# A two-block transformer kernel: nine of the memory's key and value products in rounded parts, and the convolution's sum one product later

## The chip, the cores and the metric

The kernel runs on one core of one Trainium2 chip. The metric is the device time of one execution in microseconds (us). TensorE (PE) multiplies, VectorE (DVE) and ScalarE (ACT) work elementwise, SyncE (SP) issues the weights' DMAs. PSUM has eight banks of 128 x 512 floats.

## The reference, cut to what matters

Two blocks of a model of width 1024 on 512 tokens. The first has two layers, each with a mixer, a cross attention to a memory of 256 tokens, and a SwiGLU FFN. The change lies in a layer where the mixer ends and the memory's keys and values are computed:

```
y_att  = mla_group(...)                 # 8 heads, chunk-causal softmax, heads of 64
y_conv = conformer_conv_group(...)      # GLU, depthwise conv of 31 taps, LayerNorm over 512 channels, silu
x = layer_norm(ALPHA * x + concat([y_att, y_conv]) @ mix_w_o, ...)
kv = (mem @ xa_w_kv).reshape(B, M, 2, XA_HEADS, XA_HEAD_DIM)   # mem: 256 x 1024, xa_w_kv: 1024 x 2048
k, v = kv[:, :, 0], kv[:, :, 1]
```

All in float32. The second block (a gated delta network and 16 experts) is not touched.

## The kernel before

Everything is feature-major: a tensor of 1024 features and n tokens is 8 tiles of 128 partitions by n. The order of the work on each engine is written out by hand; engines meet through counting semaphores (`signal`), one step for each instruction of a kind.

**Rounded products.** A plain float32 matmul is two records in the trace. Most large products of the kernel are instead made of three matmuls in the rounded type fp32r: weights and inputs are split in a high part (a copy that rounds) and a low part (the difference), and `split_product` adds high x high, high x low and low x high for each of the 8 k. Here the split weights are made by ACT (high) and DVE (low).

**The stage.** In each layer PE runs a loop over 8 heads. For head h: `turn_probs(h, (0, 1))`, the scores of head h + 2, in some heads `modulation_rows` (a small product for the second block, weights streamed through the ring), `turn_probs` of tiles 2 and 3, in even heads `sums_across` (the reciprocals of the softmax sums of two heads, spread to bank 4), then `values(h)`. ACT takes the exponentials of head h + 1 ahead of head h's evictions (`turned_probs`, L2558), and copies bank 4 to mixT (L2573). DVE takes the maxima (`maximum`), the reciprocals, and between them single taps of the depthwise convolution (`convolve(n)`: 4 x 31 = 124 taps a layer, L3352, the first of each tile L3349). Product 0 of the memory stands in head 6.

After the heads PE runs `memory_product(1)` to `(11)` (`product`, L1197): products 0 to 7 give the key tiles (128 features x 256 memory tokens), 8 to 11 the values (two token tiles by 512, 512, 512 and 256 columns; the last 256 come later). Between them stand `conv_sum` (behind product 6; it needs all 124 taps), `conv_variance` (behind 8) and the spread of the reciprocal (behind 9, L1218). Then comes `residual(0, ...)`, the output projection by mix_w_o, in rounded parts: its inputs `m_split` are made of mixT by DVE (`split_half`, attention half and convolution half), its weights by `high(n)` on ACT (L2612) and `low(n)` on DVE (L3211).

**Memory.** `ring` has three slots; the key and value weights are chunks 10, 11 and 12 (`C_XKV`), which SP loads when PE has given slots back (`give_back`, `used`). In layer 0 the last of four modulation rows gives back three slots at once. The last value weights, `w_vlast`, go to the arena behind the last head. `raw`, slot 2, takes the chunks of mix_w_o once product 7 is done.

Of the kernel before, what the change touches and what calls it, by code (L numbers as in the profile page):

```python
# [80 lines left out]
RING_MODS = (4, 5)  # L81
LATE_MODS = {(0, 1): 4, (0, 2): 5, (1, 1): 5}
# [5 lines left out]
MIX_SPLIT = 2 * (CT - 1) + 4  # L88
HALF = FT // 2
# [102 lines left out]
def build(nc, A, out, debug=None):  # L192
    with ExitStack() as ctx:
# [146 lines left out]

        kr_raw = probsT[:, 0, :]
# [95 lines left out]
        mw_hi, mw_lo = signal("split_weights_hi", MIX_SPLIT + SPLIT_CHUNKS), signal("split_weights_lo", MIX_SPLIT + SPLIT_CHUNKS)  # L437
        f_hi, f_lo = mw_hi.after(MIX_SPLIT), mw_lo.after(MIX_SPLIT)
# [451 lines left out]

        def norm_banks(i):

            return (2, 3, 4, 5, 4) if i == 2 else (0, 1, 2, 6, 7)
# [237 lines left out]
        def _(pe):  # L1131
# [46 lines left out]
            for l in range(DEPTH):  # L1178
# [79 lines left out]
                def split_product(bank, weights, rhs, n, need):  # L1258

                    for k in range(n):  # L1260
                        need(k)
                        for wp, rp in ((0, 0), (0, 1), (1, 0)):
                            mm = pe.matmul(bank[:, :], weights(wp, k), rhs(rp, k), start=(k == 0 and wp == rp),  # L1263
                                           stop=(k == n - 1 and wp == 1))
                            if k == 0 and wp == rp:
                                say_spent(mm)
# [10 lines left out]
                def residual(i, n0, rhs, ready):  # L1277


                    for t in range(KT):  # L1280
                        if t >= 4:
                            pe.wait_ge(z_ok.sem, z_ok.at(l, i * KT + t - 3))
                        split_tile(ps[(6, 7, 4, 5)[t % 4]], n0, t, rhs, ready).then_inc(res_mm.sem, 1)
# [219 lines left out]
                def memory_product(n):  # L1503
# [30 lines left out]
                for h in range(HEADS):  # L1534
# [3 lines left out]
                    if 1 <= h < RING_MODS[l]:  # L1538
                        modulation_rows(h)
# [8 lines left out]
                    if h < RING_MODS[l]:  # L1548
                        modulation_turn(h)
# [3 lines left out]
                for n in range(1, 12):  # L1553
# [3 lines left out]
                    if n == 6:  # L1557
# [812 lines left out]
        def _(act):  # L2370
# [37 lines left out]
            for l in range(DEPTH):  # L2408
# [151 lines left out]

                act.wait_ge(kcopy.sem, kcopy.at(l, 1))
                exps(0)
                for h in range(HEADS):
# [3 lines left out]
                    if h < RING_MODS[l]:  # L2567
                        act.wait_ge(mod_rows.sem, mod_rows.at(l, h + 1))
                        A1(gates[:, h % 2, 0:P], mod_row(l, h)[:, 0:P], ACT.Copy).then_inc(mod_row_ev.sem, 1)
                    turned_probs(h, (2,))  # L2570
                    if h % 2 == 0:
                        act.wait_ge(rec_mm.sem, rec_mm.at(l, h // 2 + 1))
                        A1(mixT[:, h // 2, :], ps[4][:, :], ACT.Copy).then_inc(rec_ev.sem, 1)  # L2573
                    turned_probs(h, (3,))
# [53 lines left out]

                for n in range(1, 12):
                    memory_copy(n)  # L2630
                    if n == 6:
# [3 lines left out]
                    if n == 9:  # L2635
                        conv_silu()
                    if n == 9:
                        high(0)

                high(1)  # L2640
# [523 lines left out]
        def _(dve):  # L3164
# [31 lines left out]
            for l in range(DEPTH):  # L3196
# [20 lines left out]
                def add_in(i, t):  # L3217
                    dve.wait_ge(res_mm.sem, res_mm.at(l, i * KT + t + 1))
                    V.scalar_tensor_tensor(out=zT[:, t, :], in0=xT[:, t, :], scalar=ALPHA,
                                           in1=ps[((6, 7, 0, 1) if i == 2 else (6, 7, 4, 5))[t % 4]][:, :],  # L3220
# [39 lines left out]
                def add_shifted(i, t):  # L3260
# [13 lines left out]
                    bank = ps[((6, 7, 0, 1) if i == 2 else (6, 7, 4, 5))[t % 4]][:, :]  # L3274
# [118 lines left out]
                for t in range(CT):  # L3393
# [5 lines left out]
                    convolve(6 if t < CT - 1 else 16)  # L3399
# [49 lines left out]

                for h in range(HEADS):  # L3450
# [567 lines left out]
```

## Time and profile before

| | us |
|---|---|
| runs | 2459.09 median of 3 (2456.24 to 2461.99) |
| profiled execution | 2459.64, its span 2457.8 |
| TensorE busy | 2406.1 (98%) |
| VectorE busy | 1245.3 (51%) |
| ScalarE busy | 792.1 (32%) |
| mean granted TensorE clock | 0.996 of full speed |

The page also gives the chain of work that ended last, followed back from the last instruction. The groups by form tell one shape of an instruction from another, with count, busy time and mean. The timeline merges neighbouring instructions of a line; in brackets stands the idle time of the engine before them and what ended it. Times are from the span's start. PE is matmuls, PEld weight loads; the end of a matmul is modelled, so that starts are the better measure of its pace.

### The profile page before, as it was taken

What the parts mean: (1) busy time and instruction counts of PE and PEld (TensorE: products, weight loads), DVE (VectorE), ACT (ScalarE), POOL (GpSimd) and SP (SyncE); (2) the same over time, 40 slices, a digit from 0 to 9 for tenths busy, and PEclk for the clock granted to TensorE, in tenths of its full rate; (3) what the DMA queues carried; (4) which work ended last, traced back from release to release, by engine and by line L of the source; (5) the groups of instructions that cost most, each with busy time, mean ns of one, the idle gap of its engine ahead of it and who ended that gap; (6) DMA issues with size and microseconds to landing.
All of it is one profiled execution on the core that took longest, in us unless ns stands there. A gap on an engine that the chain in (4) does not pass through costs nothing.

```text
span 2457.8 us, 35670 instructions
## 1 busy us (share of the span) xinstructions
PE 2406.1 (98%) x15406; PEld 1721.0 (70%) x15406; DVE 1245.3 (51%) x1826; ACT 792.1 (32%) x1284; POOL 173.5 (7%) x117
## 2 busy tenths in 40 slices
PE   9999999999999999999999999999999999999998
PEld 6566877888887757687788888787899754444332
DVE  6884746433336887555633434687566431112122
ACT  4452534222224353343422322526333441111111
POOL 0000000000000000000000000190344010000000
PEclk9999999999999999999999999999999999999999
DMA  4352222323334233322332322211100289999998
GB/s 171 98 180 95 75 97 69 96 85 104 103 110 141 65 138 138 103 69 90 100 97 83 112 88 84 95 70 69 37 3 3 104 321 426 427 426 426 427 427 342
DMA packets 248819, 380.70 MB, mean 155 GB/s; under 512 B 21945, under 2 KB 187094, under 8 KB 224982
## 3 DMA queue, kind: packets, MB, share of 16 engines
q1 hardware_dynamic: 248316, 378.31, 41.9%
q8 instruction: 122, 2.00, 0.3%
q14 instruction: 35, 0.29, 0.0%
q10 hardware_dynamic: 346, 0.11, 0.0%
HBM read 376.28 MB, written 2.10 MB: 154 GB/s over the span
## 4 chain that ended last, share of the span: by engine, by line
PE 89%; DMA 6%; DVE 2%; ACT 2%; SPq 1%; issue 1%; DVEq 0%; ACTq 0%
PE banks L1263 41%; PE banks L2242 10%; PE banks L1197 6%; PE banks L1752 4%; PE banks L1896 4%; DMA ring<-in_w_gate 3%; PE banks L1246 2%; PE banks L2088 2%; PE banks L1617 1%; PE banks L1250 1%; PE banks L1591 1%; DMA arena<-in_w_gate 1%; PE banks L1432 1%; PE banks L2188 1%; PE banks L2226 1%; PE banks L1495 1%
## 5 line engine op out<-in xcount | busy, mean ns | idle before, releaser
L2612 ACT ACTIVATE w_hi<-ring 128x2048 fp32r<-128x2048 f32 (+1 forms) x100 | 174.5, 1745 | 424.0 <-PE banks L1263 424.0
L1263 PE MATMUL banks<-ffn_x_hi,w_lo 128*128 128x512 f32 x640 | 249.2, 389 | 0.0
L1263 PE MATMUL banks<-ffn_x_lo,w_hi 128*128 128x512 f32 x640 | 249.2, 389 | 0.0
L1263 PE MATMUL banks<-ffn_x_hi,w_hi 128*128 128x512 f32 x640 | 249.2, 389 | 0.0
L3211 DVE TENSOR_TENSOR w_lo<-ring,w_hi 128x2048 fp32r<-128x2048 f32 (+1 forms) x96 | 198.7, 2069 | 63.0 <-ACT w_hi L2612 61.8
L3352 DVE SCALAR_TENSOR_TENSOR arena<-arena,taps 128x512 f32<-128x512 f32 x240 | 174.0, 773 | 1.1
L3572 DVE TENSOR_TENSOR squares<-gates,banks 128x512 f32<-128x512 f32 x44 | 30.3, 688 | 275.5 <-PE banks L1263 262.3
L1263 PE MATMUL banks<-ffn_hidden_hi,w_hi 128*128 128x512 f32 x352 | 138.5, 393 | 0.0
L1263 PEld LDWEIGHTS banks<-ffn_x_lo,w_hi 128*128 128x128 f32 x640 | 120.2, 188 | 24.9
L1263 PEld LDWEIGHTS banks<-ffn_x_hi,w_lo 128*128 128x128 f32 x640 | 120.2, 188 | 24.9
L1263 PEld LDWEIGHTS banks<-ffn_x_hi,w_hi 128*128 128x128 f32 x640 | 120.2, 188 | 24.8
L1263 PE MATMUL banks<-ffn_hidden_hi,w_lo 128*128 128x512 f32 x352 | 137.2, 390 | 0.0
L1263 PE MATMUL banks<-ffn_hidden_lo,w_hi 128*128 128x512 f32 x352 | 137.1, 390 | 0.0
L3968 DVE SCALAR_TENSOR_TENSOR gates<-gates,tap_rows,banks 128x512 f32<-128x512 f32 x16 | 12.0, 747 | 227.6 <-PE banks L2242 196.4
L2242 PE MATMUL banks<-arena,zT 128*64 128x512 f32 x448 | 103.0, 596 | 2.1 <-DMA arena<-in_w_gate 1.0
L2242 PE MATMUL banks<-ring,zT 128*64 128x512 f32 x432 | 98.5, 597 | 2.5 <-DMA ring<-in_w_gate 2.0
L1197 PE MATMUL banks<-arena,ring 128*128 128x256 f32 (+1 forms) x352 | 98.0, 438 | 0.0
L1896 PE MATMUL banks<-arena 64*64 64x64 f32 x2688 | 87.3, 222 | 0.7 <-ACT arena L2883 0.7
L1197 PEld LDWEIGHTS banks<-arena,ring 128*128 128x128 f32 x352 | 66.7, 190 | 30.4 <-issue 24.2
L1896 PEld LDWEIGHTS banks<-arena 64*64 64x64 f32 x2688 | 83.4, 137 | 5.0 <-issue 1.5
L2242 PEld LDWEIGHTS banks<-arena,zT 128*64 128x64 f32 x448 | 30.6, 137 | 65.1 <-issue 58.3
L1263 PEld LDWEIGHTS banks<-ffn_hidden_lo,w_hi 128*128 128x128 f32 x352 | 66.1, 188 | 14.0 <-issue 0.5
(571 smaller groups left out, 4695.4 us busy)
## 6 DMA issues: line engine op xcount, KB each, us to landing
ring<-in_ffn_w_in SPq DMA_DIRECT2D x88, 512.0 KB, 4.8
arena<-in_w_gate SPq DMA_DIRECT2D x28, 1024.0 KB, 21.1
arena<-in_w_up SPq DMA_DIRECT2D x28, 1024.0 KB, 21.4
ring<-in_w_gate SPq DMA_DIRECT2D x27, 1024.0 KB, 22.3
ring<-in_w_up SPq DMA_DIRECT2D x27, 1024.0 KB, 21.5
ring<-in_w_down SPq DMA_DIRECT2D x24, 1024.0 KB, 17.5
arena<-in_w_down SPq DMA_DIRECT2D x24, 1024.0 KB, 20.3
ring<-in_w_mod SPq DMA_DIRECT2D x18, 1024.0 KB, 7.0
```

The lines of the kernel that those rows point to most:

```text
L1197: mm = pe.matmul(bank[0:m, 0:width], weights(k), rhs(k), start=(k == 0), stop=(k == n - 1))
L1246: pe.matmul(ps[outs[o]][:, :], weights(o, wp, k), rhs[0][:, k, :], start=(k == 0 and wp == 0), stop=False)
L1250: mm = pe.matmul(ps[outs[o]][:, :], weights(o, 0, k), rhs[1][:, k, :], start=False, stop=(k == KT - 1))
L1263: mm = pe.matmul(bank[:, :], weights(wp, k), rhs(rp, k), start=(k == 0 and wp == rp), stop=(k == n - 1 and wp == 1))
L1752: mm = pe.matmul(out, wt[:, k, :], z[:, k, :], start=(k == 0 and i == 0), stop=(k == KT - 1 and i == 2))
L1896: mm = pe.matmul(units_of(bank)[rows, un, :], lhsT(un, rows), rhs(un, rows), start=True, stop=True)
L2088: mm = pe.matmul(bank, w_parts[wp], r_parts[rp], start=(k == DH and wp == rp), stop=(k == DH - 1 and wp == 1))
L2242: mm = pe.matmul(out, tokens, weights[:, n * 512:(n + 1) * 512], start=first, stop=last)
L2612: nc.scalar.activation(hi[:, 0:m], raw[n % 2][:, 0:m], ACT.Copy).then_inc(f_hi.sem, 1)
L3211: ins = V.tensor_tensor(lo[:, 0:m], raw[n % 2][:, 0:m], hi[:, 0:m].bitcast(F32), ALU.subtract)
L3352: ins = V.scalar_tensor_tensor(out=acc, in0=x, scalar=c, in1=acc, op0=ALU.mult, op1=ALU.add)
L3572: V.tensor_tensor(whole, gates[:, t % 2, :], ps[2 * (t % 4) + 1][:, :], ALU.mult)\
```

## The change

Products 1 to 7 (keys) and 8 and 9 (the first 512 value columns) become rounded products of three parts. The memory (`mem_x`, 2048 elements a partition) and eleven pieces of the weights (1024 each, `mem_part(1)` to `(11)`; piece 0 stays plain) are split: ACT makes the high parts (`memory_high`), DVE the low ones (`memory_low`, `memory_x_low`). The low parts lie on the raw weights in the ring, the high ones where the latents, queries and keys of the heads were and in zT, where the probabilities were. The value pieces' high parts lie on those of products 1 to 3. Since `m_split` lies on the memory's parts, `split_half(0)` goes behind product 9 on DVE.

Around it: `conv_sum` and the squares go from behind product 6 to behind product 7. In even heads tile 2 is turned ahead of the modulation rows, with `sums_across` and ACT's copy of bank 4; at head 6 this puts them ahead of product 0. In layer 0 modulation rows 3 go from head 3 to head 4 (`ROW_HEADS`). DVE takes the reciprocal of head h - 1 ahead of head h's maxima. Its taps: 7 more before the head loop, 2 instead of 4 in heads 5, 6 and 7, then 7 and 18 instead of 13 and 13. ACT makes the memory's high part in head 5, between the evictions of tiles 2 and 3, and pieces 1 and 2 in head 6. The projection's banks are 4, 6, 7, 5 instead of 6, 7, 4, 5, each with its own wait (`mixed_bank`); ACT makes `high(0)` ahead of `conv_silu` and `high(1)` ahead of product 11's eviction.

```diff
@@ new
+ROW_HEADS = ({0: 0, 1: 1, 2: 2, 4: 3}, {0: 0, 1: 1, 2: 2, 3: 3, 4: 4})
+        mem_x = [nc.alloc_sbuf_tensor_at(f"memory_{part}", [P, KT, MEM], F32R, offset=arena_at + 4 * lo).ap()
+                 for part, lo in (("hi", 0), ("lo", 12 * S))]
+        def res_bank(i, t):
+            return ((4, 6, 7, 5), (6, 7, 4, 5), (6, 7, 0, 1))[i][t % 4]
@@ PE, memory_product
-                    if n < 8:
+                    if 1 <= n < 8:
+                        pe.wait_ge(mem_lo.sem, mem_lo.at(l, n + 1))
+                        parts = mem_part(n)[1:]
+                        mm = split_product(bank, lambda i, k: parts[i][:, k], lambda i, k: mem_x[i][:, k, :], KT, lambda k: None, MEM)
+                    elif n < 8:
                         mm = product(bank, lambda k: wkv[:, k, (n % 4) * P:(n % 4 + 1) * P], lambda k: memT[:, k, :], width=MEM)
+                    elif n < 10:
+                        t = n % 2
+                        mm = split_product(bank, lambda i, k: mem_x[i][:, k, t * P:(t + 1) * P],
+                                           lambda i, k: (mem_v_hi, mem_w_lo[2])[i][:, k, :], KT,
+                                           lambda k: pe.wait_ge(mem_lo.sem, mem_lo.at(l, 8 + k // 2 + 1)))
@@ PE, heads
-                    if 1 <= h < RING_MODS[l]:
-                        modulation_rows(h)
+                    if h % 2 == 0:
+                        turn_probs(h, (2,))
+                        sums_across(h // 2)
+                    if h and h in ROW_HEADS[l]:
+                        modulation_rows(ROW_HEADS[l][h])
                     if h == HEADS - 2:
                         pe.wait_ge(sc_exp.sem, sc_exp.at(l, (HEADS - 1) * ST + 1))
                         memory_product(0)
-                    turn_probs(h, (2,))
-                    if h % 2 == 0:
-                        sums_across(h // 2)
+                    if h % 2:
+                        turn_probs(h, (2,))
                     turn_probs(h, (3,))
@@ PE, products
-                    if n == 6:
+                    if n == 7:
                         conv_sum()
@@ PE, projection
-                pe.wait_ge(mod_in.sem, mod_in.at(l, RING_MODS[l]))
-                pe.wait_ge(xkv_ev.sem, xkv_ev.at(l, 12))
-                residual(0, N_MO, m_split, lambda k: part_ready(pe, m_part, l, k))
+                def mixed_bank(t):
+                    if t in (1, 2):
+                        pe.wait_ge(xkv_ev.sem, xkv_ev.at(l, 10 + t))
+                    if t == 3:
+                        pe.wait_ge(mod_in.sem, mod_in.at(l, RING_MODS[l]))
+                        pe.wait_ge(cmul.sem, cmul.at(l, CT + 1))
+                residual(0, N_MO, m_split, lambda k: part_ready(pe, m_part, l, k), mixed_bank)
@@ ACT
+                def memory_high(i):
+                    act.wait_ge(loaded[slot(C_XKV + i // 4)], 32 * ring_loads(l, C_XKV + i // 4))
+                    raw_w, hi, _ = mem_part(i)
+                    A1(hi, raw_w, ACT.Copy).then_inc(mem_hi.sem, 1)
+                    if h == HEADS - 2:
+                        act.wait_ge(sc_mm.sem, sc_mm.at(l, ST * HEADS))
+                        for i in range(1, 3):
+                            memory_high(i)
+                    if h % 2:
+                        turned_probs(h, (2,))
+                    if h == HEADS - 3:
+                        act.wait_ge(up_mm.sem, up_mm.at(l, 16))
+                        A1(mem_x[0], memT, ACT.Copy).then_inc(mem_hi.sem, 1)
                     turned_probs(h, (3,))
+                memory_high(3)
+                act.wait_ge(pt_mm.sem, pt_mm.at(l, ST * HEADS))
+                for i in range(4, 8):
+                    memory_high(i)
                 for n in range(1, 12):
                     memory_copy(n)
+                    if n == 3:
+                        for i in range(8, 12):
+                            memory_high(i)
@@ DVE
-                    convolve(6 if t < CT - 1 else 16)
+                    convolve(7 if t < CT - 1 else 20)
+                    if h:
+                        reciprocal(h - 1)
                     for t in range(ST):
                         maximum(h * ST + t)
-                        if t == 1 and h >= 1:
-                            reciprocal(h - 1)
-                        if h >= 2:
+                        if 2 <= h < 5 or h >= 5 and t % 2 == 0:
                             convolve(1)
                 pair_out(HEADS // 2 - 2)
                 reciprocal(HEADS - 1)
-                convolve((CT * TAPS - sum(taps_done)) // 2)
+                memory_x_low()
+                for i in range(1, 3):
+                    memory_low(i)
+                convolve(7)
+                memory_low(3)
                 pair_out(HEADS // 2 - 1)
+                for i in range(4, 8):
+                    memory_low(i)
                 convolve(CT * TAPS - sum(taps_done))
-                split_half(0, m_part, mixT, m_split)
+                for i in range(8, 12):
+                    memory_low(i)
@@ DVE, behind the convolution's output
+                dve.wait_ge(xkv_mm.sem, xkv_mm.at(l, 10))
+                split_half(0, m_part, mixT, m_split)
+                low(N_MO)
                 dve.wait_ge(cout.sem, cout.at(l, CT))
                 split_half(1, m_part, mixT, m_split)
-                low(N_MO)
                 low(N_MO + 1)
```

## Rows read from the trace of the kernel before

**Rows 1.** The page: engines' busy time, and the chain by engine.
```profile
PE 2406.1 (98%) x15406; PEld 1721.0 (70%) x15406; DVE 1245.3 (51%) x1826; ACT 792.1 (32%) x1284; POOL 173.5 (7%) x117
...
PE 89%; DMA 6%; DVE 2%; ACT 2%; SPq 1%; issue 1%; DVEq 0%; ACTq 0%
```

**Rows 2.** Stretches: length; busy (records) of PE, PEld, DVE, ACT, POOL; clock; DMA.
```profile
181.25:202.08 20.83, 20.83 (x98) 18.38 (x98) 14.57 (x26) 1.92 (x5) 0.00 (x0) 1.00 0.29 102
202.08:205.51 3.43, 3.43 (x9) 1.52 (x8) 0.00 (x0) 0.38 (x1) 0.00 (x0) 1.00 0.00 0
...
208.96:215.92 6.96, 6.96 (x17) 2.85 (x15) 0.00 (x0) 0.38 (x1) 0.00 (x0) 1.00 0.68 230
215.92:216.93 1.01, 1.01 (x33) 0.81 (x32) 0.00 (x0) 0.60 (x1) 0.00 (x0) 1.00 1.08 384
...
223.91:224.79 0.88, 0.88 (x9) 0.88 (x8) 0.00 (x0) 0.67 (x2) 0.00 (x0) 1.00 0.00 0
224.79:235.91 11.12, 10.49 (x34) 5.94 (x33) 8.52 (x13) 7.13 (x9) 0.00 (x0) 1.00 0.00 0
181.25:235.91 54.66, 54.03 (x225) 36.59 (x225) 26.53 (x44) 15.40 (x25) 0.00 (x0) 1.00 0.22 77
953.16:1007.80 54.64, 54.03 (x225) 36.58 (x225) 26.55 (x44) 15.38 (x25) 0.00 (x0) 1.00 0.23 77
```

**Rows 3.** PE's timeline in layer 0's output projection: start, duration, line, operands.
```profile
241.02 0.39 PE L1263 MATMUL banks<-mixed_lo,w_hi 128*128 128x512 f32 x1
...
246.46 0.39 PE L1263 MATMUL banks<-mixed_lo,w_hi 128*128 128x512 f32 x1
```

**Rows 4.** Groups by form: weight loads from 181 to 246.
```profile
L1218 PEld LDWEIGHTS banks<-std,spreads 128*128 128x128 f32 x8 | 1.1, 192 | 0.5 <-issue 0.5
```

**Rows 5.** Groups by form, ACT and DVE, 20 to 260: count, busy, mean.
```profile
L2612 ACT ACTIVATE w_hi<-ring 128x2048 fp32r<-128x2048 f32 x4 | 7.6, 1909 | 12.8 <-PE banks L1263 12.8
...
L2454 ACT ACTIVATE mix_w_hi_glu<-ring 128x1024 fp32r<-128x1024 f32 x6 | 6.0, 1052 | 0.0
...
L3245 DVE TENSOR_TENSOR mix_w_lo<-ring,mix_w_hi_glu 128x1024 fp32r<-128x1024 f32 x6 | 7.2, 1220 | 0.6 <-ACT mix_w_hi_glu L2454 0.6
L3211 DVE TENSOR_TENSOR w_lo<-ring,w_hi 128x2048 fp32r<-128x2048 f32 x3 | 6.9, 2286 | 2.5 <-ACT w_hi L2612 2.5
```

**Rows 6.** DVE's timeline, layer 0; bracketed: idle time before, and its releaser.
```profile
84.35 0.69 DVE L3401 TENSOR_TENSOR arena<-arena,cosT 64x512 f32<-64x512 f32 x1 [3.74 <-ACT arena L2496]
...
173.66 8.67 DVE L3352 SCALAR_TENSOR_TENSOR arena<-arena,taps 128x512 f32<-128x512 f32 x13
...
205.71 2.48 DVE L3412 SCALAR_TENSOR_TENSOR arena<-banks,arena 128x512 f32<-128x512 f32 x4 [9.83 <-PE banks L1411]
```

**Rows 7.** Timeline of PE, layer 0, heads 4 to 6.
```profile
161.91 1.09 PE L1454 MATMUL banks<-consts,stat 128*64 128x128 f32 x16 [0.35 <-DVE stat L3433]
...
169.99 0.98 PE L1443 MATMUL banks<-consts,zT 128*128 128x128 f32 x7
170.81 3.62 PE L1197 MATMUL banks<-arena,ring 128*128 128x256 f32 x16
...
176.37 0.32 PE L1466 MATMUL banks<-arena 128*64 128x128 f32 x1 [0.44 <-ACT arena L2573]
```

**Rows 8.** Timeline of ACT, layer 0, heads 3 and 5 to 7.
```profile
149.65 0.37 ACT L2538 ACTIVATE zT<-banks,stat 128x128 f32<-128x128 f32 x1
...
151.90 0.98 ACT L2558 ACTIVATE arena<-banks 128x512 f32<-128x512 f32 x2
...
168.55 0.55 ACT L2558 ACTIVATE arena<-banks 128x256 f32<-128x256 f32 x2 [1.73 <-PE banks L1443]
...
172.52 0.97 ACT L2558 ACTIVATE arena<-banks 128x512 f32<-128x512 f32 x2
```

**Rows 9.** SP's key weight issues; DMA GB/s in 40 slices, 156 to 184.
```profile
157.32 7.02 SPq L959 DMA_DIRECT2D ring<-in_xa_w_kv  x6
...
GB/s 23 0 12 59 117 410 398 418 404 410 404 413 410 401 415 413 410 401 415 407 410 404 413 407 410 395 228 23 20 0 0 0 0 0 0 0 0 29 111 348
```

More of the change, by code:

```diff
@@ L88 @@
 MIX_SPLIT = 2 * (CT - 1) + 4
+MEM_SPLIT = 12
 HALF = FT // 2
@@ L339, in mix_w, with mem_part @@
             return hi, mix_w_lo[c][:, :, cols]
+        mem_x = [nc.alloc_sbuf_tensor_at(f"memory_{part}", [P, KT, MEM], F32R, offset=arena_at + 4 * lo).ap()
+                 for part, lo in (("hi", 0), ("lo", 12 * S))]
+        mem_k_hi = [nc.alloc_sbuf_tensor_at(f"memory_k{j}_hi", [P, 4, KT, P], F32R, offset=arena_at + 4 * lo).ap()
+                    for j, lo in enumerate((4 * S, -KT * S))]
+        mem_v_hi = nc.alloc_sbuf_tensor_at("memory_v_hi", [P, KT, 512], F32R, offset=arena_at + 4 * 4 * S).ap()
+        mem_w_lo = [nc.alloc_sbuf_tensor_at(f"memory_w{j}_lo", [P, KT, 512], F32R, offset=ring_at + 4 * ((C_XKV + j) % NSLOT) * SLOT).ap()
+                    for j in range(3)]
+        def mem_part(i):
+            if i < 2 * 4:
+                cols = slice(i % 4 * P, (i % 4 + 1) * P)
+                return w(C_XKV + i // 4, 0, KT, 512)[:, :, cols], mem_k_hi[i // 4][:, i % 4], mem_w_lo[i // 4][:, :, cols]
+            ks = slice(2 * (i - 8), 2 * (i - 8) + 2)
+            return w(C_XKV + 2, 0, KT, 512)[:, ks], mem_v_hi[:, ks], mem_w_lo[2][:, ks]
         kr_raw = probsT[:, 0, :]
@@ L436, in build @@
         raw_in = [sem(f"split_chunk{i}_in") for i in range(2)]
-        mw_hi, mw_lo = signal("split_weights_hi", MIX_SPLIT + SPLIT_CHUNKS), signal("split_weights_lo", MIX_SPLIT + SPLIT_CHUNKS)
-        f_hi, f_lo = mw_hi.after(MIX_SPLIT), mw_lo.after(MIX_SPLIT)
+        mw_hi, mw_lo = [signal(f"split_weights_{part}", MIX_SPLIT + MEM_SPLIT + SPLIT_CHUNKS) for part in ("hi", "lo")]
+        mem_hi, mem_lo = mw_hi.after(MIX_SPLIT), mw_lo.after(MIX_SPLIT)
+        f_hi, f_lo = mw_hi.after(MIX_SPLIT + MEM_SPLIT), mw_lo.after(MIX_SPLIT + MEM_SPLIT)
         b3w_hi, b3w_lo = mw_hi, mw_lo
@@ L1256, in first_four, with split_product @@
                     part(range(2, 4), range(KT // 2, KT))
-                def split_product(bank, weights, rhs, n, need):
+                def split_product(bank, weights, rhs, n, need, width=S):
                     for k in range(n):
@@ L1262, in split_product @@
                         for wp, rp in ((0, 0), (0, 1), (1, 0)):
-                            mm = pe.matmul(bank[:, :], weights(wp, k), rhs(rp, k), start=(k == 0 and wp == rp),
+                            mm = pe.matmul(bank[:, 0:width], weights(wp, k), rhs(rp, k), start=(k == 0 and wp == rp),
                                            stop=(k == n - 1 and wp == 1))
@@ L1275, in split_tile, with residual @@
                                          lambda i, k: rhs[i][:, k, :], KT, ready if t == 0 else lambda k: None)
-                def residual(i, n0, rhs, ready):
+                def residual(i, n0, rhs, ready, before=lambda t: None):
                     for t in range(KT):
@@ L1282, in residual @@
                             pe.wait_ge(z_ok.sem, z_ok.at(l, i * KT + t - 3))
-                        split_tile(ps[(6, 7, 4, 5)[t % 4]], n0, t, rhs, ready).then_inc(res_mm.sem, 1)
+                        before(t)
+                        split_tile(ps[res_bank(i, t)], n0, t, rhs, ready).then_inc(res_mm.sem, 1)
                         if t == 1:
@@ L2635, in _ @@
                     if n == 9:
+                        high(0)
                         conv_silu()
-                    if n == 9:
-                        high(0)
-                high(1)
+                    if n == 10:
+                        high(1)
                 residual_squares(0, N_MO)
@@ L3273, in add_shifted @@
                     dve.wait_ge(pre_ok.sem, pre_ok.at(l, i * KT + t + 1))
-                    bank = ps[((6, 7, 0, 1) if i == 2 else (6, 7, 4, 5))[t % 4]][:, :]
+                    bank = ps[res_bank(i, t)][:, :]
                     V.scalar_tensor_tensor(out=zT[:, t, :], in0=zT[:, t, :], scalar=1.0 if i == 2 else ALPHA, in1=bank,
```

29 lines of the change are left out of this document (19 added, 10 removed).

## The prediction, made before the changed kernel ran

> **What bounds the kernel now.** I read the page first, for who is busy: TensorE has work for 98% of the span and 89% of the chain that ended last is TensorE [rows 1]. So time moves only if TensorE's own stream in the touched stage gets shorter or gets a hole. The stage is the same in both layers: head loop, twelve memory products, output projection. The table of stretches cuts its second part, from the first key product after the last head to the first matmul of the output projection [rows 2]: 54.66 us in layer 0, 54.64 in layer 1, granted clock 1.00, and TensorE idle 0.63 us in it, in the last stretch (11.12 us, 10.49 busy), just ahead of the projection. VectorE is busy for 26.5 us of the 54.7 and ScalarE for 15.4. That is the room that the added copies and subtractions have. Then come the timelines of the other engines: where VectorE stands when the convolution's sum is taken (it waited 9.83 us for it [rows 6]), and how ScalarE and TensorE hand the last heads to each other [rows 7, 8].
>
> **Two prices of a product.** A plain fp32 matmul is two records, each with its own weight load. Six key products (8 matmuls with 256 columns each) take 20.83 us [rows 2], 3.47 each. A value product with 512 columns takes 6.96 [rows 2]. A rounded matmul of 512 columns is one record; 24 of them go by from 241.02 to 246.46 [rows 3], so one each 0.227 us. A value product in three rounded parts is 24 x 0.227 = 5.45 us, 1.51 less.
>
> The rounded matmul of 256 columns isn't in this trace. From below: half of 0.227 is 0.113, and the spread of a vector issues 8 records, each with a 128-column load, in 0.88 us, one each 0.110 [rows 2, 4]; so loads of this size can follow each other at 0.110 under as much streaming. From above: 0.192, the whole record of such a load [rows 4], if nothing of it hides behind a stream that is only half as long as now. Between them a case of 0.135, a point that I choose: a third of what separates 0.107 from 0.192 shows. I take 0.117, near the low end, because the spread's records are the nearest row. A key product is then 24 x 0.117 = 2.81 us, 0.66 less than now.
>
> The Trainium skill speaks against this: its page "TensorE: Matmul & The Clock Gate" (Part 3, The mechanism) says a weight load overlaps matmuls in flight only when the row group differs, and here every load fills the whole array. The trace disagrees: the spread's whole-array loads last 192 ns in the record and follow at 110 ns [rows 2, 4]. With the page's load of columns / 1.2, 107 ns, added to each stream, a key product would be an estimated 24 x 0.22 = 5.3 us and the kernel over 30 us slower. The sum here does without it.
>
> **After the heads, per layer.** Seven key products at 2.81: 19.7. The convolution's sum: 3.43 [rows 2]; it moves one product back and costs the same. Two value products: 10.9. The variance 1.01 and the spread 0.88, unchanged. Products 10 and 11 stay plain: 10.5 of the last stretch's 11.12 us. The hole of 0.63 goes, because the projection's first tile now takes bank 4 and doesn't wait for the last eviction. Sum 46.4 for 54.66: a gain of 8.2 us.
>
> **Is VectorE ready?** It gets x_low (2048 wide, 2.29 us) and eleven subtractions of 1024 (1.22 us by record, about 1.14 in a row) [rows 5]: 2.3 + 12.5 = 14.8 us, of which 10.3 stand ahead of the convolution's last tap. It gives back: the split of the attention half (4 casts, 4 subtractions, 3.8 us) goes behind the spread, and seven taps go ahead of the heads, where it waits 3.74 us before the key rotation [rows 6], so they cost nothing (without that cover 7 x 0.66 = 4.6 us). Written out, in times of layer 0: reciprocal of head 7 near 171.4, x_low to 173.7, low 1 and 2 (they wait for ScalarE's copies, below) to 177.2, seven taps to 181.9 (13 take 8.67, rows 6, 0.66 each), low 3, the last pair's output, low 4 to 7 to 188.9, 18 taps to 200.8. TensorE, starting product 1 at 181.7 (next part), is through product 7 at 201.4. So the convolution's sum starts with 0.6 us to spare: VectorE is nearly the bound there, and a faster narrow matmul than 0.117 gives little more. Behind it low 8 to 11 run to 205.5, under the sum (to 204.9) and the first half of product 8, which takes them two k at a time; centring ends at 208, the variance is asked for at 210.3. Splits of both halves and low(N_MO) end near 226 to 230, the projection starts near 228 with the first half and takes the second from 230.9 on. ScalarE's copies (2048 wide 1.91, 1024 wide 1.05 [rows 5]) stand in 15.4 us of work in 54.7 [rows 2]. In order: copies 1 and 2 by 175.8, under product 0; 3 to 7 from 180.7 to 186, which holds product 1's eviction back, but product 5 is the first to need it, at 193; 8 to 11 behind product 3's eviction, 190.4 to 194.6. The first half's split now waits for product 9, and low(N_MO) and the second half are queued behind it; both engines have 10.5 us of plain products for that. All fit, the tightest by 0.6.
>
> **In the heads.** Gain: now the reciprocals' spread is followed at once by values that wait 0.44 us for ScalarE's copy of it [rows 7], some 0.6 us with the pipe's drain. It now has modulation rows (1.9 us of TensorE) behind it at heads 2 and 4, and product 0 at head 6. Head 4 of layer 0 also loses a wait of 0.35 us for the reciprocal [rows 7], whose instruction moves ahead of head 6's maxima. I count 0.6 at head 2 and 0.95 or 0.6 at head 4: 1.55 us in layer 0, 1.2 in layer 1.
> Loss: the 2048-wide copy of the memory (1.91 us) stands on ScalarE at head 5 between the evictions of tiles 2 and 3. ScalarE was idle 1.73 us [rows 8], but ahead of tile 2, not behind it. Queued behind the copy are tile 3's eviction (head 5's last values wait, about 1 us) and head 7's exponentials. These take 2.2 us with nothing in the way (149.65 to 151.90 with a short wait [rows 8]); now they end at 172.5 because VectorE's taps stretch them. With half of the taps gone VectorE would be 0.8 earlier, but ScalarE starts them only at 170.7: end 172.9. Product 0, which ran from 170.81 [rows 7] while TensorE waited for this, is now behind the turn of tile 2 and the reciprocals' spread, both of which need them. TensorE's turn of head 6 starts at about 171.0 (169.99 before [rows 7]), is done at 171.7, and waits until head 6's first tile is evicted at 173.4. Product 0 starts at 174.8 and product 1 at 183.3 instead of 181.25, before the gains above. Net of the 0.6 that head 6 saves, 2.0 us are lost. Bounds: 0, if exponentials or TensorE run later than I think anyway, and 3.5, a whole product 0 without its cover.
> Moving modulation rows 3 to head 4 in layer 0 moves the release of all three weight chunks: SP's six transfers start at 157.32 [rows 9] and would start at about 162.8. A chunk is 1024 x 512 floats, 2.1 MB. By the slices (0.7 us each) some 0.1 MB move before 159.5 and then 0.41 MB per us [rows 9], so the first chunk was in at 164.3, 7.0 us after its issue. It would be in at 169.8; product 0 wants it at 173.2, ScalarE's first copy at 174. Hidden, with over 3 us to spare; the third chunk lands near 181 and is wanted at 190. w_vlast goes with the last head as before.
>
> **The sum.** 2 x 8.2 = 16.4 after the heads; in the heads 1.55 + 1.2 - 2 x 2.0 = -1.25. Together -15.2 us. Against the profiled execution's 2459.64 (span 2457.8 and 1.8 around it): 2444.4; the median of the runs is 0.55 lower. I say 2444.
>
> **Rivals.**
> - Narrow rounded matmuls at 0.135: +24 x 0.018 x 7 = 3.0 us per layer, 2450.4. For it: no row of this width. Against: the spread's 0.110.
> - VectorE late at the convolution's sum: each microsecond beyond the spare 0.6 goes onto the path, twice. With 14.8 us of added work and subtractions at 1.4 instead of 1.14, or low 1 and 2 held up by ScalarE in the heads, 3 us a layer: 2450. For it: the 0.6. Against: it waited 9.83 us there before.
> - The heads lose a whole product's cover, 3.5 us a layer: 2447.5. This lies inside the forecast's range.
> - Slower: narrow loads don't overlap. If each rounded matmul of 256 columns takes the load's whole record, 0.192 [rows 4], a key product is 4.61, +12.6 us a layer: 2469.6. It decides from 24.3 (seven plain) + 1.51 x 2 + 0.63 - 0.6 over 168 matmuls, 0.163 us per matmul. Against: the spread; for it only that a plain matmul streams for twice as long behind each load. The skill's rule named above is this one's stronger form.
> - The change makes no difference: it would take 0.16 per narrow matmul or a VectorE 7 us late; no row points there.
>
> **Chances.** Forecast 0.67 (2440 to 2448.5), narrow matmuls at 0.135 0.10, VectorE late 0.14, slower 0.05, no difference 0.04. What the measurement tells from no change is 0.2%, 4.9 us. Faster holds the first three, 0.91; same 0.04; slower 0.05. The range takes in the second and third: from 2439 (0.110 per matmul, no loss in the heads, both limited by the convolution's sum) to 2452, a little beyond their two times.
>
> **What would show it.** In the page TensorE's key products as one line of about 336 rounded 128x256 records, pitch 0.11 to 0.12; from product 1 to the projection 46 to 47 us in both layers; VectorE's wait of 9.83 before the first centring gone, and TensorE's idle before the convolution's sum under 1 us; no idle before the projection; a hole of 1 to 2 us in head 6 ahead of turn tile 2, put down to ScalarE's L2558 eviction. Wrong would be: pitch of 0.14 and above, a hole before the convolution's sum, low(N_MO) after the end of product 11, or product 0 waiting for its weights.

## Result: 2446.18 us, and the profile after

The changed kernel takes 2446.18 us (median of 4 runs, 2443.97 to 2447.30), beside 2460.38 us for the kernel before in the same comparison (4 runs, 2456.24 to 2461.99). The ratio is 0.9944, 95% interval 0.9932 to 0.9956: 14.2 us less. Predicted were 2444, between 2439 and 2452, faster at 0.91. The profiled execution took 2443.97 us, its span 2442.2.

The page of the changed kernel, its parts on busy time and on the chain by engine, answers to [rows 1]:

```profile
PE 2391.0 (98%) x15550; PEld 1723.4 (71%) x15550; DVE 1276.2 (52%) x1850; ACT 816.2 (33%) x1308; POOL 173.5 (7%) x117
...
PE 90%; DMA 5%; DVE 3%; ACT 2%; issue 1%; SPq 0%; DVEq 0%; ACTq 0%
```

TensorE has 144 more records and 15.1 us less work. VectorE has 30.9 us more and ScalarE 24.1 us more, and neither shows in the time: they stay at 52% and 33% of the span. The next table cuts the products of the changed kernel into stretches (columns as in [rows 2]); it starts with product 1 at 179.74 and ends with the first matmul of the projection, and the last two rows are the whole stage in each layer:

```profile
179.74:199.98 20.24, 20.24 (x169) 20.24 (x169) 20.18 (x29) 9.54 (x14) 0.00 (x0) 1.00 0.29 105
199.98:203.01 3.03, 3.03 (x10) 1.35 (x9) 3.03 (x3) 0.38 (x1) 0.00 (x0) 1.00 0.02 5
203.01:208.99 5.98, 5.98 (x26) 4.49 (x24) 2.60 (x5) 2.37 (x4) 0.00 (x0) 1.00 0.68 219
208.99:210.00 1.01, 1.01 (x33) 0.81 (x32) 0.00 (x0) 0.60 (x1) 0.00 (x0) 1.00 1.05 369
210.00:215.58 5.58, 5.58 (x28) 4.62 (x25) 0.95 (x1) 1.96 (x3) 0.00 (x0) 1.00 0.21 74
215.58:216.47 0.89, 0.89 (x9) 0.89 (x8) 0.00 (x0) 0.69 (x2) 0.00 (x0) 1.00 0.00 0
216.47:226.61 10.14, 10.14 (x35) 5.93 (x33) 9.94 (x17) 8.32 (x8) 0.00 (x0) 1.00 0.03 4
...
179.74:226.61 46.87, 46.87 (x298) 38.32 (x297) 36.70 (x53) 23.86 (x32) 0.00 (x0) 1.00 0.27 91
945.20:992.09 46.89, 46.89 (x298) 38.34 (x297) 36.71 (x53) 23.86 (x32) 0.00 (x0) 1.00 0.27 91
```

The reader is to see three things. The stage took 54.66 and 54.64 us [rows 2] and takes 46.87 and 46.89. TensorE is busy for all of it: the hole of 0.63 us ahead of the projection is gone, and none came ahead of the convolution's sum. And in the first row VectorE is busy for 20.18 of 20.24 us: it is nearly as full as TensorE there. Its own timeline says how far it is from being late (answers to [rows 6]):

```profile
186.57 12.01 DVE L3417 SCALAR_TENSOR_TENSOR arena<-arena,taps 128x512 f32<-128x512 f32 x18
198.50 4.62 DVE L3519 TENSOR_TENSOR memory_w_lo<-ring,memory_v_hi 128x1024 fp32r<-128x1024 f32 x4
203.62 2.49 DVE L3477 SCALAR_TENSOR_TENSOR arena<-banks,arena 128x512 f32<-128x512 f32 x4 [0.49 <-PE banks L1436]
```

The last tap ends at 198.58, the sum starts on TensorE at 199.98: 1.4 us of room. The wait of 9.83 us ahead of the centring is 0.49.

Where the time between the two profiled executions lies, from landmarks on TensorE (first score of the heads, product 1, projection): heads 59.42 to 59.93 us in layer 0 and 61.15 to 62.07 in layer 1 (+0.51, +0.92); products -7.79 and -7.75; from the projection of layer 0 to the heads of layer 1 656.10 to 656.52 (+0.42, of which 0.32 is a wait for a transfer, 0.75 us where it was 0.43); the rest after layer 1 +0.11. What lies ahead of layer 0's heads is 2.02 us shorter, 119.81 for 121.83. The sum is -15.6.

Those 2.02 us lie in work that no edit of the change touches. TensorE's timeline at the start of the kernel before, and under it that of the changed kernel, the same work:

```profile
26.17 0.30 PE L1290 MATMUL banks<-consts,par_rows 128*128 128x128 f32 x1 [0.96 <-DMA tap_rows<-in_conv_dw_w]
...
28.52 0.63 PE L1263 MATMUL banks<-mix_x_hi,mix_w_hi_glu 128*128 128x512 f32 x1
28.95 0.63 PE L1263 MATMUL banks<-mix_x_lo,mix_w_hi_glu 128*128 128x512 f32 x1
```

```profile
25.75 0.30 PE L1315 MATMUL banks<-consts,par_rows 128*128 128x128 f32 x1 [0.45 <-DMA tap_rows<-in_conv_dw_w]
...
28.36 0.39 PE L1287 MATMUL banks<-mix_x_hi,mix_w_hi_glu 128*128 128x512 f32 x1
28.59 0.40 PE L1287 MATMUL banks<-mix_x_lo,mix_w_hi_glu 128*128 128x512 f32 x1
```

In the execution of before a transfer came half a microsecond later, and then the rounded matmuls went at a pitch of 0.43 us instead of 0.23: the granted clock was 0.76 in 24 to 31 us, and 1.00 in the changed kernel's. Without this the two profiled executions differ by 13.6 us, close to the 14.2 of the medians. Whether the late start is a matter of that one execution or of the kernel before isn't shown: only one execution of it was profiled, and all nine profiled executions with the changed code (this one and the eight experiments) start their heads at 119.5 to 119.9 us, with a granted clock of 1.00 in that window.

### The profile page after: what moved, and what is told of

Its sections match the earlier page's. It is cut to its first block, busy times and chain, and to the rows that moved or that the text cites. A ratio compares the mean times of both kernels' runs of the same rounds, so it can differ in the third digit from the quotient of the medians.

```text
span 2442.2 us, 36024 instructions
## 1 busy us (share of the span) xinstructions
PE 2391.0 (98%) x15550; PEld 1723.4 (71%) x15550; DVE 1276.2 (52%) x1850; ACT 816.2 (33%) x1308; POOL 173.5 (7%) x117
## 3 DMA queue, kind: packets, MB, share of 16 engines
q8 instruction: 123, 2.02, 0.3%
## 4 chain that ended last, share of the span: by engine, by line
PE 90%; DMA 5%; DVE 3%; ACT 2%; issue 1%; SPq 0%; DVEq 0%; ACTq 0%
PE banks L1287 44%; PE banks L2284 11%; PE banks L1794 4%; PE banks L1938 4%; PE banks L1221 3%; PE banks L1270 2%; DMA ring<-in_w_gate 2%; PE banks L2130 2%; PE banks L1659 1%; PE banks L1274 1%; DMA arena<-in_w_gate 1%; PE banks L1633 1%; PE banks L2268 1%; PE banks L1457 1%; PE banks L2230 1%
## 5 line engine op out<-in xcount | busy, mean ns | idle before, releaser
L2795 ACT ACTIVATE gates<-banks 128x512 f32<-128x512 f32 x44 | 26.4, 600 | 149.4 <-PE banks L1287 137.2
L1287 PEld LDWEIGHTS banks<-ffn_hidden_lo,w_hi 128*128 128x128 f32 x352 | 66.1, 188 | 14.1 <-issue 0.5
L1287 PEld LDWEIGHTS banks<-ffn_hidden_hi,w_hi 128*128 128x128 f32 x352 | 66.1, 188 | 14.1 <-issue 0.5
```

The costliest lines, as they stand in the source:

```text
L1287: mm = pe.matmul(bank[:, 0:width], weights(wp, k), rhs(rp, k), start=(k == 0 and wp == rp), stop=(k == n - 1 and wp == 1))
L2795: nc.scalar.activation(gates[:, t % 2, :], ps[2 * (t % 4)][:, :], ACT.Silu).then_inc(ffn_act.sem, 1)
```

## Experiments

All start from the changed kernel; each was compared with the kernel before on the same chip, which there took 2458.24 us (e1 to e4) or 2457.60 us (e5, e6, e7, e9). Medians of different comparisons are better held against each other by their ratios. Parts that an edit doesn't touch differ too: the work behind layer 1's projection took from 1450.1 to 1452.8 us in the profiled executions with the changed code.

**e4_halves**: what sets the pace of a narrow rounded matmul, its stream or its weight load? Every key product from 1 to 7 is made in two halves of 128 columns, so twice as many records stream half as far.

```
-  mm = split_product(bank, ..., lambda i, k: mem_x[i][:, k, :], KT, ..., MEM)
+  for half in range(2):
+      cs = slice(half * P, (half + 1) * P)
+      mm = split_product(bank[:, cs], ..., lambda i, k: mem_x[i][:, k, cs], KT, ..., P)
```

> The changed kernel with each rounded key product made in two halves of 128 columns: 48 matmuls of 128 columns instead of 24 of 256, the same number of columns in all, twice the weight loads. Measured so far: 0.227 us for 512 columns, 0.120 for 256. Theory A (0.107 us stream at 256 columns plus a fixed 0.0133 for each rounded record, loads hidden): 0.0667 for 128 columns, 3.2 us a product, 2.3 us more in a layer, near 2451. Theory B (a load of 128 columns cannot be issued faster than about 0.110, the pace of the spread, and at 256 columns the stream is just longer than the load): 0.110 to 0.120 for 128 columns, 5.3 to 5.8 us a product, 17 to 20 us more in a layer, 2480 to 2486. If B holds, 256 columns are at the edge of being bound by the loads.

2481.31 us, ratio 1.0090 (1.0071 to 1.0108). TensorE's timeline of the changed kernel (256 columns), and under it of this one (128 columns); the second column is a record's duration, the pitch is the distance of the starts:

```profile
198.78 0.28 PE L1287 MATMUL banks<-memory_hi,memory_w_lo 128*128 128x256 f32 x1
198.90 0.28 PE L1287 MATMUL banks<-memory_hi,memory_k_hi 128*128 128x256 f32 x1
199.02 0.28 PE L1287 MATMUL banks<-memory_lo,memory_k_hi 128*128 128x256 f32 x1
```

```profile
200.01 0.27 PE L1287 MATMUL banks<-memory_hi,memory_k_hi 128*128 128x128 f32 x1
200.12 0.28 PE L1287 MATMUL banks<-memory_lo,memory_k_hi 128*128 128x128 f32 x1
200.23 0.28 PE L1287 MATMUL banks<-memory_hi,memory_w_lo 128*128 128x128 f32 x1
```

0.120 us at 256 columns and 0.112 at 128 (200.01 to 202.91 is 26 records, 0.1115 each). Half the columns save 7%: at 128 columns it isn't the stream that sets the pace, and theory A is out. What stays the same in every record is the load of a new 128x128 weight tile. For the load speaks that its record grows from 136 ns with 64 columns (the sums' loads, L1479) to 190 with 128, an estimated 108 ns for 128 columns. No run kept a weight tile for several rounded matmuls, so another cost of each rounded record of this width isn't ruled out. The stage grew to 64.22 us in layer 0; (64.22 - 46.87) / 7 + 2.88 = 5.36 us for a product of 48 records, 0.112 again.

**e2_plain_keys**: the key products in plain fp32 again, on the rounded part of the weights alone, with all copies and subtractions still made. It leaves out the low parts of weights and memory in the key products; the value products stay rounded.

```
-  mm = split_product(bank, lambda i, k: parts[i][:, k], lambda i, k: mem_x[i][:, k, :], KT, lambda k: None, MEM)
+  mm = product(bank, lambda k: parts[0][:, k].bitcast(F32), lambda k: memT[:, k, :], width=MEM)
```

> The changed kernel with products 1 to 7 as plain float32 matmuls again, on the rounded high part of the weights and the whole memory; all copies, subtractions and waits stay. It leaves out the low part of these key weights. Theory (the keys gain by TensorE's pace alone, 3.47 against 2.88 us a product; the added copies and subtractions are hidden): product 1 to projection grows from 46.9 to 51.0 us in each layer, 8.3 us in all, near 2454.5; the heads stay at 59.9 and 62.1. VectorE waits some 5.5 us for the convolution's sum. Rival (the added work costs something in the product stage by itself): more than 51.0, with holes on TensorE.

2449.93 us, ratio 0.9964 (0.9951 to 0.9976); products 50.89 and 50.90 us. So the seven rounded key products are worth 4.0 us a layer, 0.57 each, and the stage is as long as expected for plain keys (51.0) with all the added work in it. The expected 2454.5 us did not come: by the medians the run is 3.8 us slower than the changed kernel, by the ratios 4.9 with about 4 us of uncertainty, where the stage shows 8.0; the rest of this is not explained. The profiled execution's heads took 63.02 us in layer 0, 3.1 more than the changed kernel's, with the same instructions in them; the section on the hardware comes back to it.

**e3_taps_late**: the seven convolution taps that the change brings ahead of the heads go back behind them.

```
-                    convolve(7 if t < CT - 1 else 20)
+                    convolve(6 if t < CT - 1 else 16)
```

> The changed kernel with the seven taps a layer back behind the heads: 6, 6, 6 and 16 taps in the projection stage instead of 7, 7, 7 and 20, so the last run of taps is 25 instead of 18. Theory (VectorE is within 1.4 us of being the bound at the convolution's sum, where the last tap ends at 198.6 and TensorE asks at 200.0): the last tap ends 7 x 0.66 = 4.6 us later, TensorE waits 3.2 us ahead of the sum in each layer, 6.4 us in all, near 2452.6. Rival (VectorE has room, as its 52% say): no change, 2446.

2458.00 us, ratio 0.9997 (0.9986 to 1.0007): the whole gain is gone. TensorE's timeline at the sum, and the two windows ahead of and behind its start, in which the last columns are granted clock, DMA share and GB/s:

```profile
203.22 5.15 PE L1436 MATMUL banks<-arena,consts 128*128 128x512 f32 x8 [3.20 <-DVE arena L3417]
```

```profile
199.00:203.22 4.22, 1.02 (x10) 0.84 (x8) 4.22 (x8) 0.38 (x1) 0.00 (x0) 0.95 0.00 0
203.22:212.00 8.78, 8.78 (x25) 5.36 (x26) 6.88 (x8) 2.36 (x4) 0.00 (x0) 0.83 0.26 87
```

The wait is as long as foreseen, 3.20 us here and 3.16 in layer 1, but behind it the clock falls to 0.83 and the eight matmuls of the sum take 5.15 us instead of 3.60; in layer 1 they take 6.69. Products: 51.80 and 53.29 us, 4.9 and 6.4 over the changed kernel's where the wait alone explains 3.2. The forecast counted the waits alone and came out at 2452.6, 5.4 us too low. The fall isn't that of one execution: over all ten runs the mean granted clock is 0.991 to 0.995, over the changed kernel's four 0.995 to 0.997.

**e5_sum_behind_6**: the convolution's sum and ScalarE's squares stand behind key product 6, as in the kernel before.

```
-                    if n == 7:
+                    if n == 6:
                         conv_sum()
...
-                    if n == 7:
+                    if n == 6:
                         conv_squares()
```

> The changed kernel with the convolution's sum (and its squares on ScalarE) back behind key product 6. Theory A (VectorE's last tap sets the earliest place of the sum): in the changed kernel product 7 starts at 197.1 us and the last tap ends at 198.6, so the sum behind product 6 waits about 1.5 us in each of the two layers; products 46.87 -> about 48.4 us per layer, median about 2449 us, and a little more if TensorE's granted clock falls behind the wait. Rival B (the place of the sum is of no weight, product 7 runs either way and the sum finds its data): products stay at 46.9 us, median 2446.

2448.16 us, ratio 0.9960 (0.9944 to 0.9976). TensorE's timeline at the two sums:

```profile
201.47 3.67 PE L1436 MATMUL banks<-arena,consts 128*128 128x512 f32 x8 [1.42 <-DVE arena L3417]
...
972.89 3.67 PE L1436 MATMUL banks<-arena,consts 128*128 128x512 f32 x8 [1.40 <-DVE arena L3417]
```

Products 48.49 us in both layers, +1.62 and +1.60: the wait of 1.4 us and 0.2 more. Moving the sum one product back is worth what VectorE would be late by.

**e1_copy_first**: on ScalarE in head 5, the 1.90 us copy of the memory goes ahead of the exit of tile 2, into the time in which ScalarE has nothing to do.

```
+                    if h == HEADS - 3:
+                        act.wait_ge(up_mm.sem, up_mm.at(l, 16))
+                        A1(mem_x[0], memT, ACT.Copy).then_inc(mem_hi.sem, 1)
                     if h % 2:
                         turned_probs(h, (2,))
-                    if h == HEADS - 3:
-                        ...
```

> The changed kernel with one move on ScalarE in head 5: the 2048-wide copy of the memory goes ahead of the eviction of tile 2, where ScalarE was idle 1.67 us in the changed kernel's trace, instead of behind it. Theory (the two holes of TensorE in heads 5 and 6, 0.89 and 1.18 us, come from the place of the copy in ScalarE's order): the first hole goes, tile 3 is evicted some 1.5 us earlier, head 7's exponentials start earlier but their last one then waits for VectorE's maximum (its row ends at 167.3), so the second hole stays near 1.0 to 1.2; product 0 starts about 0.9 us earlier in each layer, 1.8 us less in all, near 2444. Rival (ScalarE has too much work in these heads, wherever the copy stands): both holes stay, their sum is 2.1 us a layer as now.

2446.03 us, ratio 0.9945 (0.9927 to 0.9963), where about 2444 was expected. The median can't tell this from the changed kernel, the landmarks can: heads 58.86 and 61.01 us, 1.07 and 1.06 less, and 1.2 us more behind layer 1's projection, which the edit doesn't touch. First TensorE's timeline of the changed kernel in heads 5 and 6, then of this one:

```profile
167.18 0.43 PE L1491 MATMUL banks<-arena 128*64 128x128 f32 x2 [0.89 <-ACT arena L2600]
167.54 0.98 PE L1468 MATMUL banks<-consts,zT 128*128 128x128 f32 x7
169.71 0.44 PE L1468 MATMUL banks<-consts,zT 128*128 128x128 f32 x2 [1.18 <-ACT arena L2600]
170.08 1.09 PE L1479 MATMUL banks<-consts,stat 128*64 128x128 f32 x16
171.10 3.72 PE L1221 MATMUL banks<-arena,ring 128*128 128x256 f32 x16
```

```profile
168.64 0.44 PE L1468 MATMUL banks<-consts,zT 128*128 128x128 f32 x2 [1.44 <-ACT arena L2600]
```

The wait of 0.89 us in head 5 is gone; the one in head 6 stays, a little longer.

**e6_copy_first_no_taps_7**: as e1, and VectorE does no taps between the maxima of head 7.

```
-                        if 2 <= h < 5 or h >= 5 and t % 2 == 0:
+                        if 2 <= h < 5 or 5 <= h < 7 and t % 2 == 0:
```

> The changed kernel with the memory copy ahead of the exit of tile 2 in head 5 (as in e1_copy_first), and with no convolution taps between the row maxima of head 7 (they run later, behind the halves). Theory A (the hole that was left in head 6, 1.44 us, is there because the exps of head 7 come late, and taps between the maxima take part in that): the hole shrinks to about 1.1 us or less, heads 58.86 and 61.01 -> about 58.4 and 60.6, median about 2445 us; the 1.3 us of two taps use up VectorE's spare 1.4 us. Rival B (only ScalarE's copy delays the exps): the hole stays at 1.44 us and the time at 2446. Rival C (VectorE is late at the sum): TensorE waits about 0.5 us or more ahead of the sum in each layer, median 2447 or above.

2440.27 us, ratio 0.9923 (0.9911 to 0.9935), the lowest median of all (e7's interval overlaps it): heads 58.15 and 60.30 us, another 0.71 less in each layer. About 2445 was expected; the landmarks give 3.3 us less than the changed kernel, the medians 5.9. TensorE in head 6, and VectorE at the sum:

```profile
167.81 0.44 PE L1468 MATMUL banks<-consts,zT 128*128 128x128 f32 x2 [0.72 <-ACT arena L2600]
```

```profile
184.67 13.34 DVE L3417 SCALAR_TENSOR_TENSOR arena<-arena,taps 128x512 f32<-128x512 f32 x20
197.93 4.63 DVE L3519 TENSOR_TENSOR memory_w_lo<-ring,memory_v_hi 128x1024 fp32r<-128x1024 f32 x4
```

The hole is halved. The taps that were moved end at 198.0 and the sum starts at 198.16, so VectorE's room is used up, without a wait on TensorE (rival C is out); the products grew by 0.12 us a layer, to 47.01.

**e7_copy_head_3**: the memory copy two heads earlier, no taps in head 7.

```
-                    if h == HEADS - 3:
+                    if h == HEADS - 5:
                         act.wait_ge(up_mm.sem, up_mm.at(l, 16))
                         A1(mem_x[0], memT, ACT.Copy).then_inc(mem_hi.sem, 1)
```

(this block also stands ahead of `if h % 2`, as in e1, and the line of e6 is changed)

> The changed kernel with the memory copy on ScalarE moved two heads forward (head 3, ahead of the exit of tile 2), and no taps in head 7. Theory A (both holes, 0.89 us in head 5 and 1.18 us in head 6, are made by the 1.90 us of the copy, which pushes the exps of head 7 back, and head 3 has room for it): both go, heads 59.93 -> about 58.3 us and 62.07 -> about 60.4, median about 2443 us (2441 to 2444). Rival B (the copy costs the same wherever it stands in the heads): a hole of 0.9 to 1.4 us appears in head 3 or 4 instead, median 2445 to 2446.

2441.49 us, ratio 0.9932 (0.9921 to 0.9944); heads 58.13 and 61.69 us. In layer 0 it equals e6: the hole of head 6 is 0.70 us with the copy wholly out of the way. In layer 1 a new one of 1.20 us stands in head 3:

```profile
917.11 0.32 PE L1491 MATMUL banks<-arena 128*64 128x128 f32 x1 [1.20 <-ACT arena L2600]
```

```profile
914.71 0.28 ACT L2622 ACTIVATE gates<-banks 128x128 f32<-128x128 f32 x1 [3.36 <-PE banks L1520]
914.89 1.90 ACT L2629 ACTIVATE memory_hi<-arena 128x2048 fp32r<-128x2048 f32 x1
916.69 0.55 ACT L2600 ACTIVATE arena<-banks 128x256 f32<-128x256 f32 x2
```

Layer 1 makes modulation rows in head 3. ScalarE waits 3.36 us for them, and the copy is queued behind that wait, not in it.

**e9_old_order_2_4**: in heads 2 and 4 the turn of tile 2 and the reciprocals' spread stand behind the modulation rows again.

```
-                    if h % 2 == 0:
+                    if h in (0, 6):
                         turn_probs(h, (2,))
                         sums_across(h // 2)
...
-                    if h % 2:
+                    if not (h in (0, 6)):
                         turn_probs(h, (2,))
+                        if h % 2 == 0:
+                            sums_across(h // 2)
```

(Between the two parts stand the modulation rows, and product 0 at head 6. ScalarE's exits follow in the same order.)

> The changed kernel with the order of before in heads 2 and 4 alone: turn of tile 2 and the sums across partitions behind the modulation rows on TensorE, and on ScalarE the rows' copy ahead of the exit of tile 2. Theory A (the new order in the even heads gives what the prediction counted: it takes away waits of 0.3 to 0.4 us each for the reciprocal and for the exit of a tile): heads 59.93 -> about 60.7 us and 62.07 -> about 62.8, median about 2447.5 us. Rival B (the order is worth nothing, because the rows hide the same waits): no difference of 0.2 us in a layer, median 2446.

2448.72 us, ratio 0.9957 (0.9944 to 0.9970); heads 61.25 and 63.38 us, +1.32 and +1.31. VectorE's reciprocal stays ahead of the maxima, so the wait of 0.35 us at head 4 [rows 7] stays away. The waits of 0.44 us are back in TensorE's timeline:

```profile
147.34 0.32 PE L1491 MATMUL banks<-arena 128*64 128x128 f32 x1 [0.44 <-ACT arena L2633]
...
160.86 0.32 PE L1491 MATMUL banks<-arena 128*64 128x128 f32 x1 [0.44 <-ACT arena L2633]
```

## Why the prediction held, step by step

- **The narrow rounded matmul**: 0.117 us taken, 0.120 measured; a key product 2.88 us for 2.81. That the value lay so near is in part luck. The spread's 0.110 rightly said that the loads don't forbid such a pace, and e4 goes at 0.112; but it isn't what sets the 0.120. From 512 to 256 columns the pitch falls by 0.107 us, so 256 columns stream for 0.107 and some 0.013 comes on top at both widths; 0.117 was chosen between bounds, not worked out from this. The bound of 0.192, and the rival built on it, is out: the loads' records last 192 ns but follow each other at 0.120 us under streams of 256 columns. The rule of the Trainium skill that the prediction set aside (page "TensorE: Matmul & The Clock Gate", Part 3, The mechanism) does not hold here as the prediction took it: all 336 loads fill the whole array, and the products took 2.88 us, not an estimated 5.3. The same section also names loads into a background weight buffer, which the prediction left out; the trace doesn't show which buffer a load goes to. The prediction's "over 30 us slower" is against its own forecast; against the kernel before, its sum with 5.3 us gives some 20 us, an estimate.
- **The products, 46.4 us**: 46.87 and 46.89. By stretch, predicted and measured: seven key products 19.7, 20.24; sum and value products 14.33 together, 14.59 (3.03 + 5.98 + 5.58; the cut between two products takes some of a record's drain to one side or the other); variance and spread 1.89, 1.90; the plain rest 10.5, 10.14. The gain is 7.8 us a layer for 8.2. Three terms were off, and two of them cancel in part: the key products by +0.5 (0.003 us, 168 times), sum and value products by +0.26, the plain rest by -0.36. For the rest the prediction took the 10.49 us that TensorE is recorded as busy before its hole; this ends with the last matmul's drain, 0.35 us, over which the next product starts when nothing holds it.
- **VectorE through the last tap, 0.6 us to spare**: 1.4 us measured. In the times of before (plus 2.02) the taps ended at 200.6 for 200.8, product 7 at 202.0 for 201.4: the difference is TensorE's, later by the pace of its products. That the margin is thin was right and is shown from both sides: e5 takes one product away and waits 1.42; e3 gives VectorE seven taps more (4.6 us at 0.66) and waits 3.20; e6 gives it two more (1.3) and uses it up. The bound is there, so faster key products would bring at most some 1.4 us a layer, an estimate that no run tries.
- **Heads, +0.45 and +0.8 us**: +0.51 and +0.92. The gain of the new order at heads 2 and 4 was counted as 1.2 us, and is 1.32 and 1.31 (e9). The earlier reciprocal was counted as another 0.35 in layer 0; e9 leaves it in place, and its wait of 0.35 us at head 4 is gone in the changed kernel. So the losses are 2.2 us in both layers (1.32 + 0.35 + 0.51, 1.31 + 0.92), for 2.0. They came by the ways that the prediction names. The copy's place between the exits of tiles 2 and 3 costs 1.07 us (e1). The taps that stretch head 7's maxima cost 0.71 (e6). What is left, 0.40 and 0.46, goes with the hole of 0.7 us that e6 and e7 still have, where product 0 no longer covers the exponentials, less what head 6 saves; no run moved product 0 alone. The sum closes: e6, free of copy and taps, is 1.27 and 0.85 us better in the heads than the kernel before. The prediction saw the second hole at "1 to 2 us" (1.18) and gave the first "about 1 us" (0.89).
- **Weights later**: the six transfers were issued at 160.34, which is 162.4 in the times of before, for about 162.8. Product 0 started at 171.10 with no wait for them. Hidden, as said.
- **Not foreseen**: +0.42 us between the layers, most of it a wait for a transfer, and 2.0 us at the start of the kernel, in work that the change doesn't touch. The predicted sum was -15.2 us; the products and heads together gave -14.1, and the start made the profiled executions differ by 15.6. That the median of 2446.18 lies 2.2 us above the forecast is within what the runs scatter by (2443.97 to 2447.30).

Of the rivals, VectorE late and narrow matmuls at 0.135 did not come; e3 and e5 show the first would have been dear, since a wait of 3.2 us at the sum came with 4.9 and 6.4 us in the products of the profiled execution, and with some 6 us a layer in the medians.

What stays open: whether the 0.70 us that the hole in head 6 still has without copy and taps (e7) can be taken away. ScalarE's queue there is the exits of tiles 2 and 3 of head 5, then head 7's four exponentials, about 2.0 us, then the exit that TensorE wants; in e7 this queue runs without a gap from 164.49 us on. No run put that exit ahead of the exponentials.

## What to carry to other kernels

When an engine with room takes on work, write out its timeline to the point where the bounding engine next needs it; here the cheaper products left it 1.4 us of room, and seven taps, 4.6 us, on the wrong side of that point took back the whole gain: 6.4 us by the two waits, most of the rest with falls of the granted clock. An added copy belongs into a wait that its engine already has, on the near side of it: moved by one instruction it cost 1.07 us less, moved by two heads it fell, in layer 1, behind another wait. And going from 256 to 128 columns with a new weight tile each time made the rounded matmul only 7% shorter.

## What the runs showed of the hardware

- **The pace of rounded matmuls with a fresh whole-array load each**, at a granted clock of 1.00: 0.227 us at 512 columns, 0.120 at 256, 0.112 at 128. From 512 to 256 the pitch falls by 0.107, from 256 to 128 only by 0.008.
- **A hole costs more than its length, in some executions.** The holes of 0.89 and 1.18 us in heads 5 and 6 stand alike in six profiled executions, the changed kernel's and those of e2, e3, e4, e5 and e9, in both layers. In seven of these twelve passages the second hole left the clock as it was, in five it did not (e2 in layer 0, e5 in both, e4 and e3 in layer 1). The window from 169.40 to 178.00, just behind or around the second hole, of the changed kernel, of e2 and of e5:

```profile
169.40:178.00 8.60, 7.93 (x58) 6.20 (x58) 7.38 (x8) 5.04 (x10) 0.00 (x0) 1.00 1.00 388
```

```profile
169.40:178.00 8.60, 8.22 (x35) 6.35 (x35) 6.25 (x7) 3.58 (x6) 0.00 (x0) 0.60 1.01 388
```

```profile
169.40:178.00 8.60, 8.58 (x39) 6.71 (x41) 6.25 (x7) 3.46 (x7) 0.00 (x0) 0.62 0.97 374
```

  The granted clock is 1.00 in one and 0.60 or 0.62 in the others, near the lower of the two levels (1.2 of 2.4 GHz is 0.50) for most of the window. Product 0, 3.72 us in the changed kernel, took 5.68 in e2 and 5.67 in e5, and the reciprocals' spread 1.98 for 1.09; the heads were 3.1 us longer (63.02 and 63.01 for 59.93), and in e5 again in layer 1 (65.15 for 62.07). In e4's layer 1 product 0 took 5.69, in e3's 4.41. The six passages of e1, e6 and e7, with one hole in heads 5 and 6 in place of two, kept a clock of 1.00 around it, not only at 0.72 us or less (e6, e7) but also at 1.44 (e1), so the length of that hole alone doesn't decide. Whether a fall comes seems to vary from run to run: e2 ran from 2449.26 to 2454.43 us, e5 from 2445.32 to 2454.47, e6 only from 2438.71 to 2441.10. That the clock explains all of e5's spread was not shown; only one execution of each was profiled.
